# Modulation loads as weights of two-column products, and first unit products by halves of the features, in a two-layer diffusion backbone

## The reference

```python
def modulated_norm(x, g, shift, scale):
    return rms_norm(x, g) * (1 + scale) + shift

def half_step_ffn(x, g_pre, g_post, shift, scale, gate, w_gate, w_up, w_down):
    h = modulated_norm(x, g_pre, shift, scale)
    y = (jax.nn.silu(h @ w_gate) * (h @ w_up)) @ w_down
    return x + FFN_RES * gate * rms_norm(y, g_post)

# per layer i; c and c_ctx are vectors of 1024
m_lat = (jax.nn.silu(c) @ w_mod[i] + b_mod[i]).reshape(b, N_MOD, 1, D_MODEL)
m_ctx = (jax.nn.silu(c_ctx) @ w_mod[i] + b_mod[i]).reshape(N_MOD, D_MODEL)
x = half_step_ffn(x, g[0], g[1], m_lat[:, 0], m_lat[:, 1], m_lat[:, 2], ...)
```

## Time and profile before

| | us |
|---|---|
| median of 3 runs | 1418.78 |
| lowest and highest run | 1418.36, 1424.07 |
| the profiled execution | 1414.21 |
| its span, first to last instruction | 1412.5 |
| PE, weight loads, DVE, ACT, POOL busy | 1356.1, 1136.7, 950.4, 611.0, 118.2 |

### The profile page before, as it was taken

One profiled execution on the slowest core, in us unless ns is written; L12 is line 12 of the kernel. 1 busy time (PEld: TensorE's weight loads), 2 busy tenths in 40 slices (PEclk: granted clock), 3 DMA queues, 4 the chain that ended last, 5 costly groups with the idle time before them and its releaser, 6 DMA issues.

```text
span 1412.5 us, 21742 instructions
## 1 busy us (share of the span) xinstructions
PE 1356.1 (96%) x7850; PEld 1136.7 (80%) x7850; DVE 950.4 (67%) x1395; ACT 611.0 (43%) x926; POOL 118.2 (8%) x209
## 2 busy tenths in 40 slices
PE   6999999999999999989999999999999998899997
PEld 2578888888788976578889988889876887889996
DVE  1488877888766834457788568786665685865554
ACT  2433233323546533455444464443455332644443
POOL 2100110111102102111111001100000000000000
PEclk9999999999999999999999999999999999999999
DMA  9464667677747543149888648865533433655662
GB/s 339 164 206 156 204 207 266 233 258 274 249 147 198 161 134 77 14 141 332 290 293 279 216 139 295 285 234 187 161 115 119 133 107 124 241 187 184 187 180 73
DMA packets 76360, 275.12 MB, mean 195 GB/s; under 512 B 9226, under 2 KB 9781, under 8 KB 75712
## 3 DMA queue, kind: packets, MB, share of 16 engines
q1 hardware_dynamic: 52128, 187.00, 40.1%
q0 software_dynamic: 24160, 87.12, 18.7%
HBM read 273.04 MB, written 1.05 MB: 194 GB/s over the span
## 4 chain that ended last, share of the span: by engine, by line
PE 67%; DVE 14%; DMA 8%; ACT 6%; issue 5%; DVEq 0%; SPq 0%; ACTq 0%; POOL 0%; POOLq 0%
PE gu L1406 13%; PE gu L1408 13%; PE gu L1407 13%; DMA raw<-in_wstream_dram 7%; DVE wlo L845 6%; PE acc L1467 6%; PE acc L1469 5%; PE acc L1468 5%; ACT whi L505 3%; DVE part L862 3%; PE gu L1548 1%; ACT z L539 1%; DVE act L1018 1%; PE acc L1839 1%; PE acc L1727 1%
## 5 line engine op out<-in xcount | busy, mean ns | idle before, releaser
L845 DVE TENSOR_TENSOR wlo<-raw,whi 128x1024 fp32r<-128x1024 f32 x350 | 427.5, 1231 | 206.0 <-ACT whi L505 204.6
L1406 PE MATMUL gu<-h_hi,whi 128*128 128x256 f32 (+1 forms) x1776 | 550.3, 310 | 9.4 <-DVE h_lo L960 6.9
L1408 PE MATMUL gu<-h_hi,wlo 128*128 128x256 f32 (+1 forms) x1776 | 543.0, 306 | 0.0
L1407 PE MATMUL gu<-h_lo,whi 128*128 128x256 f32 (+1 forms) x1776 | 542.9, 306 | 0.0
L505 ACT ACTIVATE whi<-raw 128x1024 fp32r<-128x1024 f32 x350 | 365.2, 1051 | 186.9 <-DMA raw<-in_wstream_dram 69.5
L1406 PEld LDWEIGHTS gu<-h_hi,whi 128*128 128x128 f32 x1776 | 340.0, 191 | 37.7 <-issue 15.8
L1407 PEld LDWEIGHTS gu<-h_lo,whi 128*128 128x128 f32 x1776 | 340.3, 192 | 17.8 <-issue 2.2
L1408 PEld LDWEIGHTS gu<-h_hi,wlo 128*128 128x128 f32 x1776 | 340.3, 192 | 14.7
L862 DVE SCALAR_TENSOR_TENSOR part<-wm,cvec,part 128x512 f32<-128x512 f32 x266 | 199.5, 750 | 6.5
L1467 PE MATMUL acc<-whi,act_hi 128*128 128x512 f32 x440 | 177.1, 402 | 6.8 <-DVE act_lo L1023 6.6
L1469 PE MATMUL acc<-wlo,act_hi 128*128 128x512 f32 x440 | 174.6, 397 | 0.0
(11 more groups left out here) (213 smaller groups left out, 1062.7 us busy)
## 6 DMA issues: line engine op xcount, KB each, us to landing
raw<-in_wstream_dram SPq DMA_DIRECT2D x350, 512.0 KB, 4.3
wm<-in_wmod_dram POOLq DMA_DIRECT2D x136, 512.0 KB, 5.5
area<-in_wmod_dram POOLq DMA_DIRECT2D x8, 512.0 KB, 8.0
z<-in_gate_rows_dram POOLq DMA_DIRECT2D x6, 512.0 KB, 6.8
gate_keep<-in_gate_rows_dram POOLq DMA_DIRECT2D x5, 512.0 KB, 6.7
area<-in_rpb_dram POOLq DMA_DIRECT2D x32, 64.0 KB, 3.5
x_lat<-in_x_in_dram SPq DMA_DIRECT2D x1, 1024.0 KB, 8.5
area<-in_ctx_in_dram SPq DMA_DIRECT2D x1, 1024.0 KB, 11.9
```

The lines of the kernel that those rows point to most:

```text
L845: nc.vector.tensor_tensor(wlo[:, u.base % RING, :], raw[:, u.base % RAW, :], whi[:, u.base % RING, :].bitcast(F32), ALU.subtract).then_inc ...
L1406: nc.tensor.matmul(out_, w_hi, x_hi, start=start, stop=False, skip_group_check=True)
L1407: nc.tensor.matmul(out_, w_hi, x_lo, start=False, stop=False, skip_group_check=True)
L1408: return nc.tensor.matmul(out_, w_lo, x_hi, start=False, stop=stop, skip_group_check=True)
```

## The change

- The four loads ahead get buffers of their own: `wm` for the first, twelve pieces for the others, eleven in the large shared area and one in `gate_keep0`. POOL issues all sixteen transfers without a wait. Their order becomes scale half 0, shift half 0, scale half 1, shift half 1.
- In `ahead`, the 128x128 blocks of the load are the weights and the two columns of `cvec` move, 4 products for each of the 8 feature blocks. The result is in columns at once, in a bank of its own (`job_p` or `mean_p`), and the row copies and `ahead_columns` are gone.
- Coefficients and shifts are applied by halves of the features: `first_coef`, `first_los(half)`, `second_los(half)`. PE's order becomes load 0, latent norm columns, load 1, context norm columns, first half of the latent products of units 0 and 1, loads 2 and 3, first half of the context products, then both second halves (`first_tiles`).
- Units 0 and 1 are split between the latent and context work of the first half; units 2 to 5 come after the second half.
- x is issued second on SP's queue, ahead of the five constants. Units 0 and 1 wait for half of load 1, unit 2 for load 3. The fifth modulation load waits for the first load's columns, the gate loads for all four.
- The squares of the first two norms write their unused output to PSUM instead of `z`.

The core of the diff:

```diff
+AHEAD_LOADS = [(1, 0), (0, 0), (1, 1), (0, 1)]
+LOADS = [(0, b, h) for b, h in AHEAD_LOADS] \
...
             sp.dma_start(cvec[:, :, :], cvec_in).then_inc(c_landed, 16)
+            sp.dma_start(x_lat[:, :, :], x_in).then_inc(x_landed, 16)
             sp.dma_start(sm[:, :], small).then_inc(const_in, 16)
...
             sp.wait_ge(wm_landed[0], 32)
-            sp.dma_start(x_lat[:, :, :], x_in).then_inc(x_landed, 16)
             sp.dma_start(x_ctx, ctx_in).then_inc(ctx_landed, 16)
-            sp.wait_ge(wm_landed[0], 64)
-            for u in range(RAW):
+            sp.wait_ge(ahead_landed[1][0], 32)
+            for u in range(2):
                 load(u, u)
+            sp.wait_ge(ahead_landed[3][1], 32)
+            load(2, 2)
...
+            for l in range(AHEAD):
+                load_ahead(l)
+            load_job(AHEAD, cols_done, lambda part_: 1)
+
+            pool.wait_ge(cols_done, AHEAD)
             load_gate(0, 2, (LAT, CTX))
...
             square(0, 0)
             square(0, 1)
-            row(0)
             square(1, 0)
             square(1, 1)
-            row(1)
-            row(2)
-            for u in range(RAW):
+            h_his(0, range(4))
+            for u in range(2):
                 split_hi(u, u, first=True)
-            row(3)
-            h_his(0, range(KT))
-            split_hi(RAW, RAW, first=True)
-            h_his(1)
+            h_his(1, HI_ORDER[:4])
+            h_his(0, range(4, KT))
+            h_his(1, HI_ORDER[4:])
+            split_hi(2, 2, first=True)
             load_table(ACT.Silu)
-            for u in range(RAW + 1, RING):
+            for u in range(RAW, RING):
                 split_hi(u, u, first=True)
...
+            for b in range(4):
+                v.wait_ge(hp_done, b + 1)
+                nc.vector.tensor_copy(z[:, 2 * b:2 * b + 2, :].rearrange("p a b -> p (a b)"), acc[:, b, :]).then_inc(xt_copied, 1)
             ahead_out(0)
             spread(1, 0)
             spread(1, 1)
...
             ahead_out(1)
-            for u in range(RAW):
+            first_coef(0, 0)
+            first_coef(1, 0)
+            first_los(0)
+            for u in range(2):
                 split(Unit(u))
+            second_los(0)
             ahead_out(2)
             ahead_out(3)
-            norm_coef(0)
-            norm_coef(1)
-            first_los()
-            split(Unit(RAW))
-            h_los(1)
-            for u in range(RAW + 1, RING):
+            first_coef(0, 1)
+            first_coef(1, 1)
+            first_los(1)
+            second_los(1)
+            for u in range(2, RING):
                 split(Unit(u))
...
             def ahead(l):
...
                 if l >= 2:
-                    pe.wait_ge(row_out, l - 1)
+                    pe.wait_ge(mod_ready, l - 1)
                 for kt in range(KT):
                     if kt % 4 == 0:
...
+                        pe.wait_ge(ahead_landed[l][kt // 4], 32)
+                    for i in range(4):
+                        ins = nc.tensor.matmul(ahead_bank(l)[:, 2 * i:2 * i + 2],
+                                               ahead_chunk(l, kt // 2)[:, kt % 2, i * P:(i + 1) * P], cvec[:, kt, :],
+                                               start=(kt == 0 and i == 0), stop=(kt == KT - 1), skip_group_check=True)
                 ins.then_inc(cols_done, 1)
+
+            def first_tiles(stream, half):
+
+                if stream == LAT and half == 0:
+                    pe.wait_ge(lo_done, 2)
+                for kt in range(4 * half, 4 * half + 4):
+                    pe.wait_ge(h_ready, first_ready(stream, kt))
+                    for k in range(2):
+                        ins = product(gu[:, k, stream * T:stream * T + T], *wblock(Unit(k), kt), h_hi[stream][:, kt, :],
+                                      h_lo[stream][:, kt, :], stream == LAT and kt == 0, kt == KT - 1)
+                        if stream == CTX and kt == KT - 1:
+                            ins.then_inc(pe_done, 1)
 
             pe.wait_ge(cs_ready, 1)
             ahead(0)
             norm_columns(0, 0)
             norm_columns(0, 1)
             ahead(1)
-            ahead_columns(0)
             norm_columns(1, 0)
             norm_columns(1, 1)
+            first_tiles(LAT, 0)
             ahead(2)
-            ahead_columns(1)
             ahead(3)
-            ahead_columns(2)
-            ahead_columns(3)
-
+            first_tiles(CTX, 0)
+            first_tiles(LAT, 1)
+            first_tiles(CTX, 1)
```

More of the change, by code:

```diff
@@ L88 @@
 GATE_SLOT = [0, 1, 0, 0, 0, 0]
-COLS_AHEAD = [(0, b, h, s) for b in range(2) for h in range(2) for s in (LAT, CTX)]
+COLS_AHEAD = [(0, b, h, s) for b, h in AHEAD_LOADS for s in (LAT, CTX)]
 BATCHES = [[job for job in jobs if job[1] not in GATE_NORM] for jobs in JOBS[:3]]
@@ L302, in tap_buffer, with ahead_bank @@
             return conv[:, idx % 4, :] if idx < 16 else x0[:, idx - 16, :]
+        def ahead_bank(l):
+            return [job_p, mean_p][l % 2]
         def inverse_bank(c):
@@ L323, in program @@
         c_landed = sem("c_landed")
-        alt_landed = [sem("wm_alt_landed0"), sem("wm_alt_landed1")]
-        wm_used, row_out, cols_done = sem("wm_used"), sem("row_out"), sem("cols_done")
+        ahead_landed = [wm_landed] + [[sem(f"ahead{l}_landed{i}") for i in range(2)] for l in range(1, AHEAD)]
+        row_out, cols_done = sem("row_out"), sem("cols_done")
         total_split, total_done = sem("total_hi_done"), sem("total_lo_done")
@@ L393, in _, with load_ahead, load_job @@
         def _(pool):
-            def load_job(l, used=None, count=None, dst=wm, sems=wm_landed):
+            def load_ahead(l):
+                for part_ in range(4):
+                    pool.dma_start(ahead_chunk(l, part_),
+                                   wmod[l][:, 2 * part_:2 * part_ + 2, :]).then_inc(ahead_landed[l][part_ // 2], 16)
+            def load_job(l, used=None, count=None):
                 for part_ in range(4):
@@ L535, in square @@
                     a.wait_ge([x_landed, ctx_landed][q], 16)
+                    junk = gu[:, :, :].rearrange("p a b -> p (a b)")
                 else:
@@ L981, in h_los, with first_los @@
                     h_lo_of(q, kt)
-            def first_los():
+            def first_los(half):
                 _, layer, stream, _, shift, _ = NORMS[0]
-                v.wait_ge(coef_done, 1)
-                v.wait_ge(mod_ready, mod_count(layer, shift, stream))
-                for kt in range(KT + 1):
-                    if kt < KT:
+                first = 4 * half
+                v.wait_ge(coef_done, coef_count(0, first))
+                v.wait_ge(mod_ready, shift_count(0, first))
+                for kt in range(first, first + 5):
+                    if kt < first + 4:
                         col = mod_column(layer, shift, stream, kt)
@@ L1442, in batch_columns @@
                 n = len(BATCHES[b])
[L1443 removed]
+                pe.wait_ge(row_out, b + 1)
                 for i in range(4):
@@ L1583, in both_turn @@
                 before = JOBS[0][2 * i - 1] if isinstance(i, int) and i else None
-                def stream_tile(k, stream):
-                    if stream == LAT:
-                        pe.wait_ge(lo_done, at_unit(u.plus(k), 1))
-                    for kt in range(KT):
-                        if k == 0:
-                            pe.wait_ge(h_ready, 8 * stream + kt + 1)
-                        ins = product(gu[:, k, stream * T:stream * T + T], *wblock(u.plus(k), kt),
-                                      h_hi[stream][:, kt, :], h_lo[stream][:, kt, :], kt == 0, kt == KT - 1)
-                    if stream == CTX:
-                        ins.then_inc(pe_done, 1)
                 def tile(k):
@@ L1607, in tile @@
                     ins.then_inc(pe_done, 1)
-                if first:
-                    for k, stream in ((0, LAT), (1, LAT), (0, CTX), (1, CTX)):
-                        stream_tile(k, stream)
-                else:
+                if not first:
                     tile(0)
```

94 lines of the change are left out of this document (46 added, 48 removed).

## The result

| | before | after |
|---|---|---|
| median of 4 runs each (lowest to highest), us | 1418.57 (1411.92 to 1424.07) | 1435.7 (1432.86 to 1436.85) |
| the profiled execution, its span, us | 1414.21, 1412.5 | 1435.41, 1433.7 |
| mean granted clock over the span | 0.990 | 0.971 |

The ratio is 1.0132 with an interval of 1.0111 to 1.0154. The change makes the kernel 1.3% slower.

A forecast was written before the change was run, and what follows sets the result against it. The start was taken as bound by PE's own order of work, not the loads. E at 74.7 less 58.0 gave +16.7 us, so 1430.9 from the profiled execution and 1435.5 from the median; forecast 1433, range 1411 to 1442.

The forecast's parts named there:

- end of load 3 (E): Time from the span's start at which PE finishes the last of the four modulation loads ahead: 74.7 us.
- The clock in the loads: In the four modulation loads, two-column products leave PE mostly at 1.2 GHz; +14 to +20 us, chance 0.78.
- Rival 2: In the loads, 128-row weight loads keep the clock high: about -2 us, the same; chance 0.13.
- The price of a pair: In the loads, one weight load with its two-column product costs 0.115 us at the upper clock, 0.213 at the lower.
- rival 3: In the loads, the clock is low but pairs keep the upper clock's 0.115 us: -3.3 us; chance 0.03.
- The norm columns: Norm-column products between loads raise the clock after about 5.1 us, taking 6.0 us a set.
- rival 5: Norm columns never lift the clock, so they take 6.8 us and loads 13.7: +25 us; chance 0.03.
- The splits behind E: After load 3, queued splits of units 2 to 5 delay silu to 14.2 us later; PE is done by 10.9.
- rival 4: Clock high and splits after load 3 not holding PE, so its own end decides: -8.7 us, faster; chance 0.03.
- Own buffers buy nothing: At the start, separate buffers for the four loads gain nothing, since loads after the first two were already hidden.
- that of x: x issued beside load 0 moves that load's start from 8.2 to 9.4 us, the middle of 8.2 and 10.7.
- From there the order of work is the old one.: Behind the first turn's silu, DVE and raw loads bound both kernels, so the start's +16.7 us carries through.

The follow-up runs named there:

- changed_again: The changed kernel unaltered, timed and profiled once more: median 1428.63 us, 1.0105 of the kernel before.
- filler: The changed kernel plus one unused 256-column product behind every four two-column products in each load: 1465.4 us, 1.0323 of the kernel before.
- splits_early: The changed kernel with the splits of units 2 to 5 moved from behind the second half to behind the first: 1426.99 us, 1.0068 of the kernel before.
- own_buffers: The kernel before with only the four loads' own buffers and x issued second on SP's queue: 1417.04 us, ratio 0.998.
- narrow_alone: The kernel before with the four loads in the two-column form, old order and buffers, plus two small edits: 1428.91 us, ratio 1.0086.
- long_form: The changed kernel with the loads' products back in the old 512-column form, row copies included: 1424.68 us, 1.0038 of the kernel before.
- long_early: The changed kernel with old-form loads, all splits earlier, unit 2 loaded without its wait and load 3's columns moved: 1406.68 us, 0.9918 of the kernel before.
- filler_dense: The changed kernel plus an unused 256-column product behind every two-column product in the loads: 1510.8 us in one run, no ratio.
- narrow_early: The changed kernel, two-column form kept, with all splits earlier and unit 2 loaded without its wait: 1425.49 us, 1.0058 of the kernel before.

## Why the prediction was right

The forecast was 1433 us with a range of 1411 to 1442 and 0.81 for slower; 1435.7 was measured. The sum, term by term, with the changed kernel's two profiled executions:

| step | predicted | after | changed_again |
|---|---|---|---|
| load 0 begins | 9.4 (8.2 to 10.7) | 10.56 | 10.52 |
| load 0 | 13.7 | 13.65 | 13.64 |
| norm columns 0 | 6.0 | 6.12 | 5.27 |
| load 1 | 11.1 | 11.24 | 9.00 |
| first-half products begin | 47.0 | 48.17 | 45.03 |
| load 2 | 11.1 | 11.53 | 10.38 |
| load 3 | 13.7 | 13.66 | 13.66 |
| end of load 3 (E) | 74.7 | 76.3 | 72.0 |
| from E to DVE's first job | 15 | 15.2 | 15.2 |
| shift of that job | 16.7 | 18.4 | 14.2 |

- **The clock in the loads** was the deciding step, and it was right. It rested on two short stretches behind which the clock had fallen, one with 16 tiny products and one in which PE was all but idle. Both held idle time, so they could not tell whether narrow products alone, without a gap, let the clock fall. The prediction was right to give it a chance and not a certainty. Rival 2, 128-row weights that hold the clock up, is out: 62.8 to 76.2 us is one unbroken stream of them at 0.50.
- **The price of a pair** was right at both levels, 0.213 and 0.115 us: 13.65/64 = 0.213 for the loads that are wholly low, and filler shows 0.12 beside 0.22 in one stream. That removes rival 3. The Trainium skill, "TensorE: Matmul & The Clock Gate", section "LDWEIGHTS (loading the stationary operand)", gives the weight load as its columns divided by 1.2 GHz with no word of the granted clock; the trace agrees with it at the upper level only and shows twice that at the lower.
- **The norm columns** lifted the clock each time, so rival 5 is out. Load 1 of changed_again is outside the terms, though: the prediction had 10.5 us with the clock up for 3.7 us, and it took 9.00.
- **The splits behind E** held PE as the prediction said (rival 4 is out): PE was done with the first tiles at 87.07 and got silu's result at 90.96. The wait was put at 3.3 us and was 3.89. The prediction took this as given; splits_early shows that it is a part of the loss (some 0.4 to 0.6%) that can be mended without touching the form.
- **Own buffers buy nothing:** right, by own_buffers. The one mis-sized term of the start is that of x: it took the place of the first load nearly wholly, 10.56 against the bound of 10.7, and I had taken the middle. That, and 0.4 us in load 2, is the 1.6 us by which E was too early.
- **"From there the order of work is the old one."** In the profiled execution 2.8 us more came behind the start: 3.3 us came back where the execution before has its low stretch at 387 us and this one has none, 4.7 were added where the attention's low clock lasted 17.1 instead of 6.8 us, and 1.9 behind that, which were not traced. The sum has no such terms, and could have none: changed_again, the same program, has 6.8 us in the attention.
- **Slips in the working,** which change nothing: from 20.06 to 55.43 PE waits for 2.5 us (1.74 and 0.73), not 3.2. With the clock up after 3.8 us and for 3.7, the terms add up to +14.9, not +14.
- **Luck.** That 1433 came within 3 us is in part luck. The start alone moved by 14.2 and by 18.4 us in two executions of the same program, on either side of the 16.7, and the stretches behind it moved by several microseconds with the clock. What the runs bear out is the mechanism and the direction, not the last 3 us.

What the sum does not separate is that its 16.7 us are two costs, and that the slow form covers a part of the other. By the pairs of kernels that differ in form alone, the form costs 0.9% in the old order (narrow_alone), 0.7 to 0.9% in the changed one and 1.4% in the mended one. By long_form against own_buffers, the new order (the halves and the place of the splits together) costs some 0.6%; these two ran on different chips, each beside the kernel before.

## What to carry to other kernels

A product with many columns of weights and few moving is priced by its weight load, and it makes PE 100% busy without holding its clock: price it at both levels of the clock before it replaces fewer, longer products, however many copies and waits it saves. When work is divided so that an engine gets to a point earlier, see what stands in the queues of the other engines at that point; here the splits had to move into the time in which ACT and DVE waited for PE. And where a change has two parts, undo each alone: here the new order, which pays in long_early, was hidden behind the form, which costs in every order.

## What the runs showed of the hardware

- **A PE that is busy without a gap can run at the lower clock:** it did for 13.4 us with 64 pairs of 128x128 weights and two columns (after, 62.8 to 76.2). In the norm columns of 128 moving columns the clock came up each time (after, at 29.5 and 46.5 us).
- **Up and down were not symmetrical** in the one execution of filler_dense: its mix ran 46.7 us at the lower level without rising, and, once the norm columns had raised the clock, stayed at the upper level through three loads, to 151 us. The thinner mix of filler fell from the upper level at 44.4 us, 6 us behind its norm columns.
- **Executions of one program differ in where the clock turns.** Load 1 of the changed kernel took 11.2 and 9.0 us in two executions. In the attention, far from the change, the low stretch lasted 6.8, 10.2 or 17.1 us in the profiled executions of this study, whatever the kernel. The first line below is a window of the changed kernel; the two below it are of the kernel before, one ahead of the rise and one behind it.

```profile
568.90:585.00 16.10, 16.10 (x29) 6.72 (x29) 6.48 (x18) 6.04 (x16) 3.71 (x5) 0.50 0.22 50
```

```profile
555.00:561.00 6.00, 6.00 (x12) 2.52 (x11) 1.40 (x3) 1.02 (x3) 0.00 (x0) 0.50 0.23 86
561.60:572.00 10.40, 10.40 (x38) 4.69 (x37) 6.40 (x18) 6.16 (x16) 6.09 (x9) 1.00 0.30 43
```

PE is busy throughout in all three. Ten more microseconds at half speed are some 5 us of work, an estimate. Runs of one kernel lie up to 8 us from their median here (narrow_early, 1417.47 to 1430.31 about 1425.49). That this spread comes from the clock was not shown.
